# The sample rows' q, k and v of heads 1 to 7 as float32 products on four groups of 32 array columns

## What is computed

```python
h = _rms_norm(x, p['g_mix'], RMS_EPS)
z = h @ p['w_in']
q = _rope(z[..., OFF_Q:OFF_K].reshape(B, T, N_HEADS, 2, HEAD_DIM), pos)
k = _rope(z[..., OFF_K:OFF_V].reshape(B, T, N_HEADS, 2, HEAD_DIM), pos)
v = z[..., OFF_V:OFF_G].reshape(B, T, N_HEADS, 2 * HEAD_DIM)
```

## Time and profile before

| what | value |
| --- | --- |
| median of 3 runs | 1674.43 us (1673.54 to 1675.08) |
| span of the profiled execution | 1673.1 us |
| TensorE busy | 1654.3 us (99%) |
| VectorE busy | 1199.4 us (72%) |
| ScalarE busy | 745.6 us (45%) |
| granted TensorE clock, mean | 0.998 |

### The profile page before, as it was taken

How to read it: one execution, slowest core, us unless ns; L and a number is a source line. 1 busy time by engine, 2 the same in 40 slices (tenths; PEclk the granted TensorE clock), 3 DMA queues, 4 the chain that set the end, 5 groups by cost and what they waited for, 6 DMA issues and landing times.

```text
span 1673.1 us, 30382 instructions
## 1 busy us (share of the span) xinstructions
PE 1654.3 (99%) x12028; PEld 1598.3 (96%) x12028; DVE 1199.4 (72%) x1989; ACT 745.6 (45%) x1524; POOL 139.5 (8%) x244
## 2 busy tenths in 40 slices
PE   8999999999999999999999999999999999999997
PEld 7899999999988999999999999999999999999997
DVE  6777777777777779776444468767666786868685
ACT  5455555555555321465312344343433543544352
POOL 3222312322210000000000000000000000000001
PEclk9999999999999999999999999999999999999999
DMA  6202202202204547575221222444444833443323
GB/s 198 64 1 76 70 14 71 77 17 61 71 1 151 180 127 240 181 261 188 89 64 58 82 89 95 140 140 140 140 140 140 308 104 128 152 149 131 107 83 127
DMA packets 153071, 194.73 MB, mean 116 GB/s; under 512 B 7642, under 2 KB 121370, under 8 KB 150874
## 3 DMA queue, kind: packets, MB, share of 16 engines
q1 hardware_dynamic: 138352, 160.59, 30.0%
q10 hardware_dynamic: 14578, 32.20, 5.3%
HBM read 148.86 MB, written 44.13 MB: 115 GB/s over the span
## 4 chain that ended last, share of the span: by engine, by line
PE 95%; DVE 3%; ACT 1%; issue 1%; DMA 0%; SPq 0%; DVEq 0%; POOL 0%; ACTq 0%; POOLq 0%
PE ps L1218 36%; PE ps L948 26%; PE ps L853 16%; PE ps L912 4%; PE ps L879 3%; PE ps L902 2%; PE ps L1271 1%; PE ps L1328 1%; PE ps L883 1%; PE ps L821 1%; PE ps L846 0%; PE ps L845 0%; PE ps L863 0%; PE ps L862 0%; PE ps L1120 0%
## 5 line engine op out<-in xcount | busy, mean ns | idle before, releaser
L853 PE MATMUL ps<-w_hi,h_hi 128*128 128x384 f32 x520 | 182.0, 350 | 0.3 <-DVE w_lo L1871 0.3
L853 PE MATMUL ps<-w_hi,h_lo 128*128 128x384 f32 x520 | 176.2, 339 | 0.0
L853 PE MATMUL ps<-w_lo,h_hi 128*128 128x384 f32 x520 | 175.4, 337 | 0.0
L1218 PE MATMUL ps<-d_hi,m_hi 128*128 128x258 f32 x784 | 158.7, 284 | 0.5 <-DVE x L2537 0.4
L1218 PE MATMUL ps<-d_lo,m_hi 128*128 128x258 f32 x784 | 159.2, 284 | 0.0
L1218 PE MATMUL ps<-d_hi,m_lo 128*128 128x258 f32 x784 | 158.2, 283 | 0.0
L1408 ACT ACTIVATE prob<-ps,nbias 128x256 f32<-128x256 f32 (+7 forms) x128 | 95.0, 742 | 78.7 <-DVE nbias L1934 76.4
L1669 ACT ACTIVATE m_hi<-m_pair 128x512 fp32r<-128x512 f32 (+1 forms) x128 | 76.9, 601 | 104.1 <-PE ps L1218 90.1
L1218 PEld LDWEIGHTS ps<-d_hi,m_hi 128*128 128x128 f32 x784 | 121.6, 190 | 1.0 <-DVE x L2537 0.6
L1218 PEld LDWEIGHTS ps<-d_hi,m_lo 128*128 128x128 f32 x784 | 122.3, 190 | 0.0
L1218 PEld LDWEIGHTS ps<-d_lo,m_hi 128*128 128x128 f32 x784 | 121.9, 190 | 0.0
(11 more groups left out here) (308 smaller groups left out, 4339.4 us busy)
## 6 DMA issues: line engine op xcount, KB each, us to landing
ff_combination_scratch<-ff_st SPq DMA_DIRECT2D x14, 1806.0 KB, 6.9
d_raw<-ff_combination_scratch ACTq DMA_DIRECT2D x21, 1032.0 KB, 7.3
w_raw<-in_w_in SPq DMA_DIRECT2D x41, 512.0 KB, 5.4
kv_pages<-in_cache_k SPq DMA_DIRECT2D x32, 512.0 KB, 5.3
kv_pages<-in_cache_v SPq DMA_DIRECT2D x32, 512.0 KB, 4.5
m_pair<-in_w_up SPq DMA_DIRECT2D x16, 1024.0 KB, 9.7
m_pair<-in_w_down SPq DMA_DIRECT2D x24, 512.0 KB, 5.2
out<-kv_st SPq DMA_DIRECT2D x16, 512.0 KB
```

What stands on the lines that cost most here:

```text
L853: mm = pe.matmul(bank[0:n, 0:3 * P], a[:, kt, toks(t)], w[:, :, kt, :], start=(kt == 0 and m == 0), stop=(kt == KT - 1 and m == 2))
L1218: mm = pe.matmul(acc[:, c], w[:, kt], a[:, kt % kts, c * CW:(c + 1) * CW], start=(opens and kt == 0 and m == 0), stop=(kt == n - 1 and m = ...
```

## The change

The samples' projection leaves step 8 and `project`. A new `project_samples(h+1)` stands at the end of step 0. `h_samples` becomes one float32 tile of 8 columns per kt, h_hi + h_lo. A head's projection is 8 products (kt = 0 to 7) of these 8 columns with the unrounded `w_raw`, in float32. Product kt writes to rows 32*(kt mod 4) and on, so it uses the array's column group kt mod 4, and each group sums two of the eight. ScalarE then makes three copies, of groups 1 to 3 (`sample_parts`, in step 1), and VectorE three adds (`sample_sum`, in step 2). `w_raw` of the next head is loaded only after `project_samples` has read it.

```diff
-            h_smp, _ = put("h_samples", [P, KT, LOW_ROW + DEC], F32R, a)
+            h_smp, _ = put("h_samples", [P, KT, DEC], F32, a)
+            z_part, _ = put("z_parts", [P, 2, 3 * P], F32, a + 4 * KT * DEC)
...
             def load_qkv(h):
                 need(sp, s_wlo, WQ * h)
+                need(sp, s_zsm, h - 1)
...
-                if hp and t == NTT:
-                    if half == 0:
-                        pe.wait_ge(s_hs, 2)
-                    for kt in range(4 * half, 4 * half + 4):
-                        both = (bank[0:LOW_ROW + DEC, 0:3 * P], h_smp[:, kt], w_hi[:, :, kt, :])
-                        small = (bank[0:DEC, 0:3 * P], h_smp[:, kt, 0:DEC], w_lo[:, :, kt, :])
...
+            def project_samples(hp):
+                bank = z_of(hp, NTT)
+                pe.wait_ge(s_exp, 16 * (hp - 1))
+                pe.wait_ge(s_hs, 1)
+                for j in range(3):
+                    pe.wait_ge(s_raw[j], 16 * (hp + 1))
+                for r in range(KT // ROW_GROUPS):
+                    for g in range(ROW_GROUPS):
+                        kt = ROW_GROUPS * r + g
+                        mm = pe.matmul(bank[g * GROUP:g * GROUP + DEC, 0:3 * P], h_smp[:, kt], w_raw[:, :, kt, :],
+                                       start=(r == 0), stop=(kt >= KT - ROW_GROUPS))
+                mm.then_inc(s_zsm, 1)
...
                 if i == 4 and h < HEADS - 1:
                     pe.wait_ge(s_zfree, z_before(h + 1, NTT))
+                    pe.wait_ge(s_zs, 3 * h + 1)
...
-                    project(h + 1, s, 1)
+                    if s < NTT:
+                        project(h + 1, s, 1)
+                    if s == 0:
+                        project_samples(h + 1)
...
+            def sample_parts(hp):
+                act.wait_ge(s_zsm, hp)
+                act.wait_ge(s_zfree, 9 * hp)
+                need(act, s_zs, 3 * (hp - 1))
+                for g, part in enumerate((z_smp, z_part[:, 0], z_part[:, 1])):
+                    done = act.activation(part[0:DEC], z_of(hp, NTT)[(g + 1) * GROUP:(g + 1) * GROUP + DEC, 0:3 * P], ACT.Copy)
+                done.then_inc(s_zl, 1)
...
             def sample_sum(hp):
-                dve.wait_ge(s_z, 9 * hp + NTT + 1)
                 dve.wait_ge(s_zl, hp)
                 dve.tensor_tensor(z_smp[0:DEC], z_of(hp, NTT)[0:DEC, 0:3 * P], z_smp[0:DEC], ALU.add).then_inc(s_zs, 1)
+                dve.tensor_tensor(z_part[0:DEC, 0], z_part[0:DEC, 0], z_part[0:DEC, 1], ALU.add).then_inc(s_zs, 1)
+                dve.wait_ge(s_zs, 3 * hp - 1)
+                dve.tensor_tensor(z_smp[0:DEC], z_smp[0:DEC], z_part[0:DEC, 0], ALU.add).then_inc(s_zs, 1)
...
-                    if s == NTT and h + 1 < HEADS - 1:
+                    if s == 2:
                         sample_sum(h + 1)
```

More of the change, by code:

```diff
@@ L95 @@
 LOW_ROW = 4 * DEC
+ROW_GROUPS = 4
+GROUP = P // ROW_GROUPS
 def need(eng, sem, value):
@@ L331, in decoder_layer @@
         s_x = [sem(f"x_in{i}") for i in range(3)]
-        s_lam_pr, s_lam_sum, s_lam_exp, s_lam = [sem(f"lam_{n}") for n in ("pr", "sum", "exp", "steps")]
+        s_lam_exp, s_lam = [sem(f"lam_{n}") for n in ("exp", "steps")]
         s_half, s_mask = sem("half_ready"), sem("mask_ready")
@@ L340, in decoder_layer @@
         s_zl, s_zs, s_hs = sem("z_sample_low"), sem("z_sample_sum"), sem("h_samples")
-        s_wq = sem("half_weights_read")
+        s_wq, s_zsm = sem("half_weights_read"), sem("z_sample_groups")
         s_vhi, s_vlo = sem("v_hi_ready"), sem("v_lo_ready")
@@ L409, in z_of, with z_done @@
             return ps[:, 3] if t == 1 else ps[:, 5] if t == NTT else bank_z
+        def z_done(hp, t):
+            return NTT * hp + (t + 1 if hp == 0 else t + 2)
         def z_before(hp, t):
@@ L707, in _ @@
             sp.wait_ge(s_wlo, W_QKV)
+            sp.wait_ge(s_zsm, HEADS - 1)
             load_a(0)
@@ L830, in project @@
                     need(pe, s_zfree, z_before(hp, t) if hp else t - 1)
-                    if hp and t == NTT:
-                        pe.wait_ge(s_exp, 16 * hp)
                     if hp and t == 1:
                         pe.wait_ge(s_qklo, 8 * hp)
-                if hp and t == NTT:
-                    if half == 0:
-                        pe.wait_ge(s_hs, 2)
-                    for kt in range(4 * half, 4 * half + 4):
-                        both = (bank[0:LOW_ROW + DEC, 0:3 * P], h_smp[:, kt], w_hi[:, :, kt, :])
-                        small = (bank[0:DEC, 0:3 * P], h_smp[:, kt, 0:DEC], w_lo[:, :, kt, :])
[L841 to L848, removed]
                 for kt in range(4 * half, 4 * half + 4):
@@ L976, in head @@
                         values(h - 1, 1 - par, NTT - 1)
-                    project(h + 1, s, 0)
+                    if s < NTT:
+                        project(h + 1, s, 0)
                     if s == NTT:
@@ L1371, in split_qkv @@
                     elif q == WQ // 2:
-                        need(act, s_z, 9 * hn)
+                        need(act, s_z, z_done(hn, -1) if hn else 0)
                     part = slice(2 * q, 2 * q + 2)
@@ L1461, in head @@
                         qk_high(h + 1, 1 - par, s - 1, turn_bank(s - 1))
-                    if s == NTT and h + 1 < HEADS - 1:
-                        sample_low(h + 1)
                     if s < NTT:
                         v_high(h + 1, 1 - par, s)
+                    if s == 1:
+                        sample_parts(h + 1)
                     if normed and s == 3:
@@ L1490, in _ @@
                     act.wait_ge(s_const, N_CONST)
-                    act.wait_ge(s_lam_sum, 1)
+                    act.wait_ge(s_lam, 2)
                     act.activation(stat[:, 34:36], stat[:, 32:34], ACT.Exp).then_inc(s_lam_exp, 1)
@@ L1502, in high @@
                 act.wait_ge(s_raw[l], RAW_QKV + 16)
-                act.wait_ge(s_z, (NTT + 1) * HEADS)
+                act.wait_ge(s_z, z_done(HEADS, -1))
                 act.activation(w_hi[:, l], w_raw[:, l], ACT.Copy).then_inc(s_whi, 1)
@@ L1537, in last_head @@
                     if s == 0:
-                        sample_low(h)
                         o_out(h - 1, 1 - par, NTT - 1)
@@ L1903, in rotate @@
                 bank = z_of(hp, t)
-                dve.wait_ge(s_z, 9 * hp + t + 1)
+                if t < NTT or hp == 0:
+                    dve.wait_ge(s_z, z_done(hp, t))
                 need(dve, s_qk, 9 * hp + t)
@@ L1908, in rotate @@
                 if hp and t == NTT:
-                    dve.wait_ge(s_zs, hp)
+                    dve.wait_ge(s_zs, 3 * hp)
                     bank = z_smp
@@ L1974, in first_samples @@
                 dve.wait_ge(s_hlo, 2 * (NTT + 1))
[L1975 to L1978, removed]
+                dve.tensor_tensor(h_smp[:], h_hi[:, :, SEQ:TOK].bitcast(F32), h_lo[:, :, SEQ:TOK].bitcast(F32),
+                                  ALU.add).then_inc(s_hs, 1)
             def head(h, par, normed, k_par):
@@ L2015, in lambda_steps @@
                 dve.tensor_copy(identb[:], ident[:]).then_inc(s_mask, 1)
-                dve.tensor_tensor(lam_pr[:], lam_in[:, 0:4:2], lam_in[:, 1:4:2], ALU.mult).then_inc(s_lam_pr, 1)
-                dve.wait_ge(s_lam_pr, 1)
-                dve.tensor_reduce(stat[:, 32:34], lam_pr[:], AX_X, ALU.add).then_inc(s_lam_sum, 1)
+                dve.tensor_tensor(lam_pr[:], lam_in[:, 0:4:2], lam_in[:, 1:4:2], ALU.mult).then_inc(s_lam, 1)
+                dve.wait_ge(s_lam, 1)
+                dve.tensor_reduce(stat[:, 32:34], lam_pr[:], AX_X, ALU.add).then_inc(s_lam, 1)
             def lambda_ready():
@@ L2022, in lambda_ready @@
                 dve.tensor_tensor(stat[:, 36:37], stat[:, 35:36], stat[:, 34:35], ALU.subtract).then_inc(s_lam, 1)
-                dve.wait_ge(s_lam, 1)
+                dve.wait_ge(s_lam, 3)
                 dve.tensor_scalar(nlam[:], stat[:, 36:37], -LAM_INIT, None, ALU.add).then_inc(s_lam, 1)
@@ L2055, in _ @@
                     lambda_steps()
-            dve.wait_ge(s_lam, 2)
+            dve.wait_ge(s_lam, 4)
             head(0, 0, False, 0)
@@ L2109, in last_head @@
                         weights(h, 0)
-                        sample_sum(h)
                         continue
```

7 lines of the change are left out of this document (2 added, 5 removed).

## The result

The kernel after takes **1680.45 us** (median of 5 runs, 1679.76 to 1682.53) against 1674.43 before: a ratio of 1.0038 with an interval of 1.0028 to 1.0049, so 6.0 us slower. Slower was forecast, and 1680.45 lies in the range, but the forecast said +20.5. The profiled execution is 1678.3 us long from first to last instruction (before 1673.1).

What follows compares the result with a forecast made beforehand. TensorE, busy 99% of the span, was taken as the bound. New products 22.4, less 11.9 recovered, plus 9.3 and 1.3 for moved adds, less 0.6, gave +20.5 on 1674.43: 1695 us, range 1679 to 1716.

Steps and rivals of the forecast that it cites:

- The sum on record: Whole kernel: new products, less removed ones, plus moved adds, less the last head's saving: +20.5 us, 1695 us.
- 9 x 0.36 = 3.2 us a head: New sample products on TensorE: 16 instructions overlap in pairs, 9 turns of 0.36 us; pairs had 50%.
- the prediction's own sign of being wrong: Wrong if the 16 instructions take under 1.7 or over 5 us, or `project(3)` starts without a wait.
- The rival of four abreast: New sample products: all four column groups run side by side, 1.5 us a head, 1683.0 in all; chance 16%.
- 1.7 of the 2.96 us come back: Head's end: removing 16 old products frees 2.96 us on TensorE, of which 1.7 is saved, seven times.
- The 1.26 of waiting ahead of the values: Head's end: 1.26 us of the removed time turns into TensorE waiting before `values(7)`, put down to `aT_lo`.
- the 0.2 for `qk_lo`: Head's end: the second four transposes share a bank with `qk_lo` and wait 0.2 us for it.
- 1.55 us in each of the six heads: VectorE's three adds before `rotate(2)` delay TensorE's `project(3)`, which waits for the `kv_st` copy, by 1.55 us a head.
- 1.3 in head 0: The same adds' delay in head 0, which has 0.7 spare: between 0.9 and 1.6, taken as 1.3 us.
- -0.6 at the last head: Last head's start: old copy and add leave, a score's 0.21 wait goes: -0.6 us, between -0.2 and -1.2.
- The drain, left out at 2.3 us: TensorE drain when the tiling mode changes: 0.16 going in and 0.16 out, 2.3 us over seven heads, not summed.

Runs made afterwards that it cites:

- e4: Kernel after with all eight sample products in one group of 32 array columns, copies and sums unchanged in number and size: 1707.24 us.
- e6: Kernel after with the sample products in two groups of 32 columns instead of four: 1690.08 us.
- e8: Kernel after with the second product of each group left out, 8 instructions a head instead of 16: 1675.72 us.
- e5: Kernel after with the same eight sample products written group by group, both of a group one after the other: 1681.3 us.
- e2: Kernel after with the sample products moved within step 0, ahead of the last values of the head before: 1683.94 us.
- e10: Kernel after with VectorE's sums in step 3 and head h + 2's sample products in step 8 of head h, head 1's left in place: 1668.33 us.
- e1: Kernel after with VectorE's three sums moved from step 2 to step 3, behind that step's maxima: 1671.96 us.

## Why the prediction was right or wrong

The sum on record was 7 x 3.2 - 7 x 1.7 + 6 x 1.55 + 1.3 - 0.6 = +20.5. By the steps measured above it is 7 x 1.48 - (7 x 2.29 - 5 x 0.35) + (6 x 1.49 + 1.06) = 10.4 - 14.3 + 10.0 = +6.1.

- **The step that failed: "9 x 0.36 = 3.2 us a head".** It measured 1.48, which takes 12.0 of the 20.5 away; the prediction's own sign of being wrong, under 1.7 us for the 16 instructions, came true with 1.41. The price of a turn was near (0.32 for 0.36, worked out from the earlier trace rows); the count was wrong, 4 turns for 9. The prediction let the second half of a product run beside the first of the next "and no more", because two halves follow each other in the program. e4, e6, after and e8 show that a group's instructions queue on that group alone, and e5 that their place in the code doesn't matter. The rival of four abreast, at 1.5 a head, is what happened; it had 16% and a time of 1683.0, 2.5 off.
- I argued against that rival by the Trainium skill's order of matmuls (TensorE: Matmul & The Clock Gate, Part 3, and in its Part 2, Step-by-step: "The MATMULs themselves stay in program order"). After and e5 don't fit it as I used it, as an order across groups, and the measurement decides. What Part 3 of that page states for packed products, a span of about one duration, agrees: a turn of four takes 0.32 us, as one instruction alone does in e4, and 5.32 to 1.48 is 3.6 times for four groups.
- **"1.7 of the 2.96 us come back": right in kind, 0.25 too little a head.** 1.95 come back in heads 1 to 5; in heads 0 and 6, 2.3. The 1.26 of waiting ahead of the values became 0.97 in three stops, of which the forecast had named two (the 0.2 for `qk_lo` measured 0.27); the third, 0.27 for GpSimd's rotated k, it didn't have. e2 and e10 show that they are empty time: products put there are free to that extent.
- **"1.55 us in each of the six heads" and 1.3 in head 0: right.** 1.49 and 1.06; the wait is the one named, `project(3)` for the `kv_st` copy, and e1 takes it away by moving the sums alone.
- **-0.6 at the last head: not seen.** The wait of 0.21 for the sum is gone, but from the last head's first score to those of its last block it is 29.62 us after and 29.49 before.
- **The drain, left out at 2.3 us.** What doesn't depend on the number of turns is 0.19 a block, 1.3 us over seven heads. The Trainium skill's drain at a change of the tiling mode (TensorEngine Tiling (Array Packing), Key Properties) would lie in it; e4, with one group, has the same 0.19, and no run separates a drain from the way into and out of a block.

The sign held because the 10 us of the sums on VectorE were sized rightly: with four abreast, the removal pays for the products, and the sums alone make the kernel slower, as e1 shows.

## What to carry to other kernels

Small products that use few array columns were priced here by the longest queue in one group of columns, so put equally many in each group; the order in which they are written cost nothing here. When they are cheap on TensorE, price what the other engines do to gather their parts: here three small sums, 1.5 us a head in front of a rotation that TensorE waits for, cost 10.0 us where the products against the removal saved 3.9, and moving them behind the next maxima gave them back. An engine that stops for a chain of others has room right behind the instruction that starts the chain: half of the products put there (e10, 0.72 of 1.48) ran for nothing.

## What the runs showed of the hardware

- **A float32 product is two instructions, and four groups of 32 columns run four of them at once**, 0.32 us a turn for 384 columns, linear from 2 to 16 turns, and at 4 turns the same in both orders of writing that were tried.
- **A stop can cost more than itself through the clock.** In e2, TensorE stood for 4.26 us at the start of head 0. The granted clock there (columns: stretch, length, busy time and count by engine, then the clock, DMA share and rate):

```profile
60.00:66.00 6.00, 1.74 (x18) 1.04 (x19) 5.52 (x15) 2.84 (x8) 0.45 (x2) 0.80 0.00 0
66.00:70.00 4.00, 4.00 (x21) 1.95 (x14) 0.53 (x2) 0.00 (x0) 0.41 (x1) 0.50 0.66 187
70.00:75.00 5.00, 5.00 (x33) 4.62 (x32) 1.16 (x4) 0.17 (x1) 0.13 (x1) 0.95 0.90 250
```

In the 4 us behind the stop the clock was 0.50, the lower level of 1.2 GHz, and the block of 16 products took 2.75 us instead of 1.48. Step 0 became 6.6 us longer (13.05 for 6.44), 2.3 more than the stop. In e10, which doesn't have this stop, the clock is 1.00 in the stretches from 60 to 66 and from 66 to 70.
